# A two-block transformer kernel on one core: its opening, its second block's gates and its square sums reordered

## What is computed

```python
def first_block(...):
    x = x + 0.5 * swiglu(rmsnorm(x, norm_ffn1_g), ffn1_w_gu, ffn1_w_down)
    x = x + hybrid_mixer(rmsnorm(x, norm_mix_g), ...)
    x = x + 0.5 * swiglu(rmsnorm(x, norm_ffn2_g), ffn2_w_gu, ffn2_w_down)
    return rmsnorm(x, final_norm_g)

def swiglu(x, w_gu, w_down):
    g, u = split(x @ w_gu)
    return (silu(g) * u) @ w_down

def second_block(x, ...):
    h = rms_norm(x, norm_mix)
    na_q, na_k, na_v, r_q, r_k, r_v, r_g = split(h @ w_in)
    na_out = neighbourhood_attention(na_q, na_k, na_v, na_rpb)   # softmax over windows
    ret = head_group_norm(bidirectional_retention(...), ret_norm_gain)
    ret_out = silu(r_g) * ret
    x = x + concat(na_out, ret_out) @ w_out
    h = rms_norm(x, norm_mlp)
    x = x + square(relu(h @ w_up)) @ w_down
    return rms_norm(x, norm_final)
```

## Time and profile before

| | |
|---|---|
| median of 3 runs | 1848.11 us (1847.36 to 1849.31) |
| time of the profiled execution | 1849.09 us |
| its span, first to last instruction | 1847.3 us |
| PE busy | 1824.0 us (99%), 8338 matmuls |
| DVE busy | 970.2 us (53%) |
| ACT busy | 623.0 us (34%) |
| moved by DMA | 176.37 MB, 95 GB/s on average |
| mean granted TensorE clock | 0.997 of full speed |

### The profile page before, as it was taken

How to read it: one execution, slowest core, us unless ns; L and a number is a source line. 1 busy time by engine, 2 the same in 40 slices (tenths; PEclk the granted TensorE clock), 3 DMA queues, 4 the chain that set the end, 5 groups by cost and what they waited for, 6 DMA issues and landing times.

```text
span 1847.3 us, 20302 instructions
## 1 busy us (share of the span) xinstructions
PE 1824.0 (99%) x8338; PEld 1502.2 (81%) x8338; DVE 970.2 (53%) x1283; ACT 623.0 (34%) x891; POOL 37.7 (2%) x38
## 2 busy tenths in 40 slices
PE   8999999999999999999999999999999999999998
PEld 6888888878888888888888888888877788888886
DVE  6434434637775534545544443456687564535354
ACT  6222222434332223323422231244656332222133
POOL 0000000000000000000000000000222000000000
PEclk9999999999999999999999999999999999999999
DMA  5232322332123322323233233223421223232322
GB/s 173 92 103 92 103 94 94 93 108 80 58 80 102 102 93 91 103 91 103 92 97 97 98 96 103 89 83 130 139 70 46 80 91 103 91 103 92 103 92 69
DMA packets 52811, 176.37 MB, mean 95 GB/s; under 512 B 6336, under 2 KB 9024, under 8 KB 52720
## 3 DMA queue, kind: packets, MB, share of 16 engines
q1 hardware_dynamic: 51520, 172.51, 28.9%
q0 software_dynamic: 448, 1.24, 0.2%
q10 hardware_dynamic: 752, 1.33, 0.2%
HBM read 170.86 MB, written 2.10 MB: 94 GB/s over the span
## 4 chain that ended last, share of the span: by engine, by line
PE 94%; DVE 3%; ACT 1%; issue 1%; DMA 0%; DVEq 0%; SPq 0%; ACTq 0%
PE ps L1351 29%; PE ps L1353 29%; PE ps L1352 28%; PE ps L1371 2%; PE ps L1372 2%; PE ps L1373 2%; DVE wl L743 1%; PE ps L1507 0%; PE ps L1381 0%; DVE tm L1167 0%; PE ps L1510 0%; PE ps L1631 0%; PE ps L1495 0%; PE ps L1642 0%; DVE X L829 0%
## 5 line engine op out<-in xcount | busy, mean ns | idle before, releaser
L1351 PE MATMUL ps<-Hhi,wh 128*128 128x512 f32 x1544 | 609.9, 395 | 7.0 <-DVE Hlo L748 7.0
L1352 PE MATMUL ps<-Hlo,wh 128*128 128x512 f32 x1544 | 602.4, 390 | 0.0
L1353 PE MATMUL ps<-Hhi,wl 128*128 128x512 f32 x1544 | 602.3, 390 | 0.0
L743 DVE TENSOR_TENSOR wl<-raw,wh 128x1024 fp32r<-128x1024 f32 (+1 forms) x320 | 389.1, 1217 | 122.1 <-ACT wh L369 120.3
L369 ACT ACTIVATE wh<-raw 128x1024 fp32r<-128x1024 f32 (+1 forms) x320 | 332.3, 1039 | 326.4 <-PE ps L1353 306.6
L1351 PEld LDWEIGHTS ps<-Hhi,wh 128*128 128x128 f32 x1544 | 290.5, 188 | 73.7 <-issue 10.8
L1352 PEld LDWEIGHTS ps<-Hlo,wh 128*128 128x128 f32 x1544 | 290.7, 188 | 62.0 <-issue 2.4
L1353 PEld LDWEIGHTS ps<-Hhi,wl 128*128 128x128 f32 x1544 | 290.6, 188 | 61.0
L1351 PE MATMUL ps<-Ahi,wh 128*128 128x512 f32 x792 | 308.9, 390 | 2.4 <-DVE Alo L1183 2.4
L1353 PE MATMUL ps<-Ahi,wl 128*128 128x512 f32 x792 | 308.8, 390 | 0.0
L1352 PE MATMUL ps<-Alo,wh 128*128 128x512 f32 x792 | 308.6, 390 | 0.0
(11 more groups left out here) (258 smaller groups left out, 1191.1 us busy)
## 6 DMA issues: line engine op xcount, KB each, us to landing
raw<-in_w_gu SPq DMA_DIRECT2D x87, 512.0 KB, 3.3
raw<-in_w_d SPq DMA_DIRECT2D x32, 512.0 KB, 3.5
raw<-in_w_up SPq DMA_DIRECT2D x32, 512.0 KB, 3.3
raw<-in_w_dn SPq DMA_DIRECT2D x32, 512.0 KB, 3.6
raw<-in_w_d SPq DMA_DIRECT2D x16, 384.0 KB, 3.1
raw<-in_w_v SPq DMA_DIRECT2D x8, 512.0 KB, 3.5
raw<-in_w_cc SPq DMA_DIRECT2D x8, 512.0 KB, 3.3
raw<-in_w_cu SPq DMA_DIRECT2D x8, 512.0 KB, 3.3
```

The source lines that it names most:

```text
L743: dve.tensor_tensor(WL[u % 3][:, 0:n], RAW[u % 3][:, 0:n], f32(WH[u % 3][:, 0:n]), ALU.subtract).then_inc(s["wl"], 1)
L1351: pe.matmul(ps, wh[:, c], hi[:, k, :], start=(k == 0), stop=False)
L1352: pe.matmul(ps, wh[:, c], lo[:, k, :], start=False, stop=False)
L1353: last = pe.matmul(ps, wl[:, c], hi[:, k, :], start=False, stop=(k == nb - 1))
```

## The change

There are three parts.

**The start.** Units 0 and 1 are multiplied side by side (`first_units`): block by block of `X`, both units' products, in two banks. Their weights lie interleaved in a new input `w_first` in four pieces of 256 KB for both units. ACT's queue issues `vec` and the first piece, SP the other three between the tiles of `X`; POOL issues `ident` only when the last tile of `X` has landed. DVE rounds the first piece itself (`tensor_copy`), ACT the others. Ahead of everything PE multiplies `ones` by `ones` four times, 256 columns each in float32, into bank 7, where nobody reads it. The first `rows_sum` moves from behind unit 1 into the middle of unit 2, and the first pair's norm, SiLU and product come behind `hi(4)`/`lo(4)`; `hi(5)`/`lo(5)` stand at the head of the next pair.

**Both feed-forward networks of the first block.** In the last eight down units the additions of squares of tile `n - 1` are made between DVE's update of `X` for tile `n` and its `Hlo` for tile `n`; the last one's come behind the loop.

**The second block's gates.** They have four buffers of their own (`G`, in the space of `RQ` and `RK`). ACT's `rows(10)` moves behind `na_e(12)` and `na_e(13)` of step 12, DVE's `ret_y(3)` to step 13. The SiLUs of gates 0 and 1 come in step 14 behind both `na_t` copies, gate 2's in step 15, gate 3's behind the loop, and so do their products and roundings. ACT's `hi` and DVE's `lo` of the third `out2` unit move behind the last gate.

```diff
@@ sp_program, pool_program
-            if n < 4:
-                sp.dma_start(RAW[0][:, 256 * n:256 * n + 256]..., src(0)[:, 2 * n:2 * n + 2, :]).then_inc(s[f"fd{n}"], 16)
-        for u in range(1, NU):
+            if n % 2 == 1 and n < 7:
+                i = n // 2 + 1
+                sp.dma_start(RAWS[:, 0:2, 256 * i:256 * i + 256], dr["w_first"][i]).then_inc(s[f"fd{i}"], 16)
+        for u in range(2, NU):
...
-        pool.dma_start(vec[:, :], dr["vec"]).then_inc(s["vec"], 16)
+        pool.wait_ge(s["x7"], 16)
         pool.dma_start(ident[:, :], dr["ident"]).then_inc(s["ident"], 16)
@@ act_program: start
+        act.dma_start(vec[:, :], dr["vec"]).then_inc(s["vec"], 16)
+        act.dma_start(RAWS[:, 0:2, 0:256], dr["w_first"][0]).then_inc(s["fd0"], 16)
         for n in range(KT):
...
             to_h(n, vc("g1", n))
+            if n % 2 == 1 and n < 7:
+                i = n // 2 + 1
+                c = slice(256 * i, 256 * i + 256)
+                act.wait_ge(s[f"fd{i}"], 16)
+                act.activation(WHS[:, 0:2, c], RAWS[:, 0:2, c], ACT.Copy).then_inc(s["fh"], 1)
-        hi(1)
+        hi(2)
@@ act_program: ffn (dve_program has the same with lo and gate)
-                    hi(u + 2)
+                    if f == 0 and j == 0:
+                        hi(3)
+                        hi(4)
+                        norm(1)
+                    elif f == 0 and j == 1:
+                        hi(5)
+                    else:
+                        hi(u + 2)
...
+                    silu(u, j)
+                    if f == 1 or j > 1:
+                        hi(u + 3)
@@ act_program: second block
-            if n in (7, 9, 11, 12):
-                rows(7 + (7, 9, 11, 12).index(n), TA[6], TA[7], TA[8])
+            if n in (7, 9, 11):
+                rows(7 + (n - 7) // 2, TA[6], TA[7], TA[8])
...
-            if n > 12:
-                rg_silu(n - 13)
...
+            if n == 15:
+                rg_silu(2)
             if n in (9, 11, 13, 15):
                 na_o((n - 9) // 2)
...
-            if n > 12:
-                rg_out(n - 13)
             if 6 <= n < 14:
                 na_e(p + 2)
+            if n == 12:
+                rows(10, TA[6], TA[7], TA[8])
+            if n == 14:
+                rg_silu(0)
+                rg_silu(1)
+                rg_out(0)
+                rg_out(1)
+        rg_out(2)
         rg_silu(3)
         rg_out(3)
+        hi(U0["out2"] + 2)
@@ dve_program: ffn
                     if g == 2:
+                        if n > 0:
+                            sums(n - 1)
                         dve.wait_ge(s["ev"], EVN[u])
                         after(n)
+            sums(KT - 1)
@@ dve_program: start
-                dve.wait_ge(s["fh"], n + 1)
-                dve.tensor_tensor(WL[0][:, c], RAW[0][:, c], f32(WH[0][:, c]), ALU.subtract).then_inc(s["fl"], 1)
+                if i == 0:
+                    dve.wait_ge(s["fd0"], 16)
+                    dve.tensor_copy(WHS[:, 0:2, c], RAWS[:, 0:2, c]).then_inc(s["f0"], 1)
+                    dve.wait_ge(s["f0"], 1)
+                else:
+                    dve.wait_ge(s["fh"], i)
+                dve.tensor_tensor(WLS[:, 0:2, c], RAWS[:, 0:2, c], f32(WHS[:, 0:2, c]),
+                                  ALU.subtract).then_inc(s["fl"], 1)
@@ dve_program: second block
-            if n in (8, 9, 11, 12):
-                ret_y((8, 9, 11, 12).index(n))
+            if n in (8, 9, 11, 13):
+                ret_y((8, 9, 11, 13).index(n))
...
             if n == 15:
+                rg_out(2)
                 na_o(3)
+                rg_lo(2)
...
-            if n > 12:
-                rg_out(n - 13)
-            if n >= 6:
+            if n == 14:
+                rg_out(0)
+                rg_out(1)
+            if 6 <= n < 15:
                 lo(u + 3)
-            if n > 12:
-                rg_lo(n - 13)
+            if n == 14:
+                rg_lo(0)
+                rg_lo(1)
...
         rg_out(3)
         rg_lo(3)
+        lo(U0["out2"] + 2)
@@ pe_program
+        def first_units():
+            for k in range(8):
+                c = slice(k * P, k * P + P)
+                pe.wait_ge(s["hh"], k + 1)
+                if k == 0:
+                    pe.wait_ge(s["f0"], 1)
+                else:
+                    pe.wait_ge(s["fl"], k // 2 + 1)
+                for i in range(2):
+                    pe.matmul(BK[BANK[i]][:, :], WH[i][:, c], Hhi[:, k, :], start=(k == 0), stop=False)
+                if k == 0:
+                    pe.wait_ge(s["fl"], 1)
+                for i in range(2):
+                    pe.matmul(BK[BANK[i]][:, :], WL[i][:, c], Hhi[:, k, :], start=False, stop=False)
+                pe.wait_ge(s["hl"], k + 1)
+                for i in range(2):
+                    last = pe.matmul(BK[BANK[i]][:, :], WH[i][:, c], Hlo[:, k, :], start=False, stop=(k == 7))
+                    if k == 7:
+                        last.then_inc(s["pe"], 1)
+
+        def first_sums():
+            pe.wait_ge(s["ss"], 7)
+            rows_sum(SS[:, :])
...
+        pe.wait_ge(s["ones"], 1)
+        for i in range(4):
+            pe.matmul(BK[7][:, 0:256], ones[:, :], ones[:, 0:1].broadcast_to([P, 256]), start=True, stop=True)
```

More of the change, by code:

```diff
@@ L180, in build @@
     Alo, oAlo = sb("Alo", [P, KT, T], F32R)
-    RAW = [sb(f"raw{i}", [P, 1024])[0] for i in range(NRAW)]
-    WH = [sb(f"wh{i}", [P, 1024], F32R)[0] for i in range(NW)]
-    WL = [sb(f"wl{i}", [P, 1024], F32R)[0] for i in range(NW)]
+    RAWS, _ = sb("raw", [P, NRAW, 1024])
+    WHS, _ = sb("wh", [P, NW, 1024], F32R)
+    WLS, _ = sb("wl", [P, NW, 1024], F32R)
+    RAW, WH, WL = ([t[:, i, :] for i in range(3)] for t in (RAWS, WHS, WLS))
     R, _ = sb("R", [P, T])
@@ L799, in a_lo, with ffn @@
             dve.tensor_tensor(Alo[:, j, :], src, f32(Ahi[:, j, :]), ALU.subtract).then_inc(s["al"], 1)
-        def ffn(f, after):
+        def ffn(f, after, sums):
             def gate(u, j):
@@ L809, in ffn @@
                     u = GU[f, g] + 2 * (j - a)
-                    lo(u + 2)
+                    if f == 0 and j == 0:
+                        lo(3)
+                        lo(4)
+                        norm(1, 1)
+                    elif f == 0 and j == 1:
+                        lo(5)
+                    else:
+                        lo(u + 2)
                     if f == 1 and j == 0:
                         norm(6, 3)
-                    if f == 1 or j > 0:
-                        gate(u, j)
-                    lo(u + 3)
-                    if f == 0 and j == 0:
-                        norm(1, 1)
-                        gate(u, j)
+                    gate(u, j)
+                    if f == 1 or j > 1:
+                        lo(u + 3)
                     dve.wait_ge(s["pe"], u + 2)
@@ L1188, in rg_out @@
         def rg_out(i):
-            g = RT[RT_G[i]]
+            g = G[i]
             dve.wait_ge(s["rgs"], i + 1)
@@ L1346, in unit @@
                     mid()
-                if u == 0 and k % 2 == 0:
-                    pe.wait_ge(s["fl"], k // 2 + 1)
                 if ready and base + k >= 0:
@@ L1386, in ffn @@
                     u = GU[f, g] + 2 * (j - a)
-                    if j == 0:
-                        unit(u, Hhi, Hlo, "hl", 16 * f)
-                        if f == 1:
-                            pe.wait_ge(s["ss"], 21)
-                            rows_sum(SS[:, :])
+                    if f == 0 and j == 0:
+                        first_units()
+                    elif f == 0 and j == 1:
+                        unit(u, Hhi, Hlo, mid=first_sums)
+                        unit(u + 1, Hhi, Hlo)
+                    elif j == 0:
+                        unit(u, Hhi, Hlo, "hl", 16)
+                        pe.wait_ge(s["ss"], 21)
+                        rows_sum(SS[:, :])
+                        unit(u + 1, Hhi, Hlo)
                     else:
                         unit(u, Hhi, Hlo)
-                    unit(u + 1, Hhi, Hlo)
-                    if f == 0 and j == 0:
-                        pe.wait_ge(s["ones"], 1)
-                        pe.wait_ge(s["ss"], 7)
-                        rows_sum(SS[:, :])
+                        unit(u + 1, Hhi, Hlo)
                 for n in range(KT):
```

55 lines of the change are left out of this document (24 added, 31 removed), and 2 rows, old and new, of the table SEMS.

## The result

The changed kernel takes 1838.21 us (median of 4, 1838.05 to 1838.37), the kernel before 1848.39 us (median of 4, 1847.36 to 1849.31). The ratio is 0.9945, with a 95% interval of 0.9928 to 0.9962. The forecast was 1837.8 us, the range 1835.3 to 1842.0.

A forecast was written before the change was run, and what follows sets the result against it. TensorE, busy for 99% of the span, was taken as the bound, so only its waits and slow clock cost time; 3.1 (start) + 1.35 (second network) + 6.85 (gates) = 11.3 us off 1849.09 gave 1837.8 us, range 1835.3 to 1842.0.

The forecast's parts named there:

- Start: Units 0 and 1: their 48 matmuls end earlier than the old 21.77, a gain of 3.1 us.
- The number of slow products: Among the first 48 matmuls, between 8 and 12 run at the half-clock pace, where the profile before had 17.
- The end of the 48: The matmuls of units 0 and 1 end at 18.7 us, before at 21.77.
- The cap by the squares: rows_sum in unit 2 needs the last addition of squares, about 20.8, so the start's gain can't pass 3.7 us.
- the prediction's own formula: With N slow matmuls in units 0 and 1, the 48 end at 5.5 + 0.2 + 0.43 N + 0.227 (48 - N).
- Second network: At its end VectorE's update period falls from 4.69 to 4.29 us and TensorE's nv wait goes: 1.35 us.
- Gates: From step 12 to out2, TensorE's waits go or shrink, so out2 starts 5.15 us earlier; 6.85 us with the clock.
- The new wait in front of `out2`: After unit 15 TensorE waits 0.9 us instead of 2.42.
- The clock term: Behind the start of out2, between 1441 and 1445, the clock stays up instead of averaging 0.57: 1.7 us.
- The table load: In the gates a load costs 1.28 us without the page's 1.38 drain, which would make out2's wait up to 2.3.
- the tail of the gates becomes the bound: Rival: the serial chain from table load to remainder keeps out2's wait and clock fall; gates give 3.5, 1841.2 us; chance 0.13.
- a slower result: Rival: TensorE waits at unit 5 and each following pair loses up to 1 us, 1858.8 us; chance 0.02.

The follow-up runs named there:

- tail: The changed kernel with na_o(3) ahead of gate 2's SiLU and product, and gate 3 taken out of its bank before the remainders of gates 0 to 2; 1837.04 us.
- rows_back: The changed kernel with rows(10) on ScalarE and ret_y(3) on VectorE back in their old places in step 12; 1839.83 us.
- only_start: The kernel before with the start part of the change alone; 1845.51 us, ratio 0.9987.
- only_sums: The kernel before with the additions of squares moved alone, in both feed-forward networks of the first block; 1846.56 us, ratio 0.9993.
- throw_on_before: The kernel before with the four throwaway products alone, behind a wait for ones, ahead of unit 0; 1847.61 us, ratio 0.9999.
- only_gates: The kernel before with the gates' part of the change alone; 1841.85 us, ratio 0.9967.
- fill_wait: The kernel before with five throwaway products on TensorE ahead of the wait in front of out2; 1847.30 us, ratio 0.9996.
- throw8: The changed kernel with eight throwaway products instead of four and its first rows_sum at the end of unit 2; 1838.40 us.

## Why the prediction was right

**Start: right in sum, off in two terms.** The first product was put at 5.5 and came at 6.03. The first piece of weights was there at 5.29 and not at 4.8, which makes 5.7 with the copy, and the step that wasn't seen at all is the ACT table load: in the changed kernel it starts when `X[0]` has landed, at 3.96, where the kernel before had it at 0.75, before any data. It put the first `Hhi` at 5.25 + 0.7. The number of slow products was put at 8 to 12 and was 8, but not for the reason given: the prediction had the clock rise once, late; in the trace it rose during the throwaways, fell at 7.3 and rose again at 10.7. That this gave a number inside the range is luck: other executions with the same start had none (`tail`) or 9 (`rows_back`). The end of the 48 was put at 18.7 and was 18.88. The gain at the next mark was 2.75 against 3.1, and it is reckoned against a start of before that was 0.4 to 0.9 us slower at that mark than in the other three traces with the old start (405.44 against 404.56 to 405.01). The cap by the squares (`rows_sum`) held: in the changed kernel TensorE came to it just in time (21.37 to 21.64 where 0.227 is the pace), in `tail` it waited 1.05 us. By the Trainium skill's figure for slow products (6 to 14, page "TensorE: Matmul & The Clock Gate", Part 1) the 8 here are ordinary and the 17 of before were many; `only_start` and `rows_back` show the same run-to-run variation (the clock up for good from 9.1 and 10.2 us). For 6 slow products the prediction's own formula gives an end of 17.8, not the 18.1 that stands there; nothing else in it hangs on that.

**Second network: right.** The period came out 0.06 us shorter than forecast (4.23 against 4.29) and the gain 1.40 against 1.35; `only_sums` has the same 1.40 in its trace.

**Gates: right step by step.** Relative to step 7, unit 13 was forecast 0.59 us earlier, and unit 14, unit 15 and `out2` 3.0, 3.46 and 5.15. The trace has 0.52, 2.87, 3.51 and 4.97. The new wait in front of `out2` was put at 0.9 and is 0.99. `rows_back` returns the two waits that the prediction gave to `rows(10)` and no others. The clock term was 1.7 against 1.63 in the trace. That the fall came from TensorE standing still is borne out by the groups of runs, but the prediction took it for certain behind a wait of 2.42 us, and it isn't: in `throw_on_before` the same wait left the clock at full. Without the fall 49.45 us pass from `out2` to the `rows_sum`, with it 50.73, in the changed kernel 49.09; so 1.3 of the 1.63 hang on whether the clock falls, and 0.35 come from gate 3's remainder being in time. `only_gates` is 6.5 us below before in the median, which fits the whole term, since most runs of before seem to have the fall; `fill_wait` is 1.0 below.

**The table load.** The rule of 2.66 us per switch (the Trainium skill, "ScalarE: Activation LUTs", "What ACT_TABLE_LOAD costs") fails here too: the load at 1424.75 takes 1.28 us and the SiLU behind it starts at 1426.04. By the page's drain of 1.38 the wait before `out2` would have been about 2.4, an estimate (0.99 and 1.38); it is 0.99.

**The sum.** The forecast took 11.3 us off the profiled execution of before, which was 0.7 us above the later median (1849.09 against 1848.39), and used the result as the median. Profile against profile the change gained 10.7 us, and median against median 10.2. So the base was 0.7 us too high and the gain 1.1 us too large for the medians; the two partly cancel, and that only 0.4 us lie between 1837.8 and 1838.21 is in part luck.

**The rivals.** That the tail of the gates becomes the bound was half true: the 0.99 us that is left is of that kind, and `tail` takes it away by order alone. No wait of the sort that a slower result needed was there: no wait on `wl` before unit 5 appears in the list.

## What to carry to other kernels

Where one engine is 99% busy, list its waits and price each by what stands right in front of the releasing instruction; here most gains of 0.5 to 3 us could be forecast from the durations of single rows, because the engines keep a written order. Work that isn't urgent (a norm's factor, a SiLU with its table load, additions of squares) belongs behind the instruction that the busy engine waits for, in a gap that the same engine already has. A wait on TensorE can cost more than its length, because the clock can fall behind it; it did so in some executions and not in others, so a single profile isn't enough to price it. Products that nobody reads can hold the clock, but their number has to be tried: six were worth 1.5 us together with a later sum, which has most of it, four 0.5 at best, and eight with that sum nothing.

## What the runs showed of the hardware that was not expected

- The throwaway products can raise the clock before there is any data: it was at full from 3.90 in the changed kernel (the last of their eight passes starts 0.28 us behind the one before it, those from the third on 0.43), from 5.44 in `tail` and from 5.49 in `throw8`. It may fall again: in the changed kernel TensorE stood still from 4.44 to 6.03, and the clock was at half from 7.3 to 10.7. It may also stay: `tail` stood still for 1.17 us before 6.01, and its clock was at full up to 1828.
- The same wait of 2.42 us with nothing to do for TensorE was followed by a clock at half in three traces (before, `only_start`, `only_sums`) and by a clock at full in a fourth (`throw_on_before`). The same kernel can so have two times: the runs of before with a mean clock of 0.997 and 0.998 have medians of 1848.50 and 1847.18 us.
- ScalarE's table load can be pushed behind a wait by what is written ahead of the first activation: at 0.75 before the change, at 3.96 behind it, 0.08 us after `X[0]` had landed; 1.28 us each. No run here tried it at an earlier place.
- The last stores can differ by 1.1 us between two executions: the span ends 7.7 us behind the start of TensorE's last product in `throw8`, and 6.1 to 6.5 us behind it in the 13 other traces.
